# Where the phases of a decoder layer meet: own buffers for one pair of weight blocks, the low parts of A on one engine, four stage buffers, waits by bank, another order of first loads

## The reference

```
z = rmsnorm(h) @ w_in                      # q | k | v | u, 1280 columns
a = windowed attention (8 heads, 2 kv heads, window 128, sinks, T5 bias)
m = pooling means of u over 2/4/8/16 positions, minus u, times w_pool, scaled
h = h + concat(a, m) @ w_out
h = h + (silu(rmsnorm(h) @ w_gate) * (rmsnorm(h) @ w_up)) @ w_down     # d_ff 2816
h = h + sigmoid(rmsnorm(h) @ w_ple_gate) * (p @ w_ple_proj)
```

## Time and profile before

| | |
|---|---|
| runs | 2328.25 us (2327.69 to 2329.66) |
| profiled execution | 2327.3 us, its span 2325.5 us, mean granted clock 0.977 |
| PE busy | 2180.4 us (94%) |
| DVE, ACT, POOL busy | 1369.0, 894.7, 395.6 us |
| edge row phase to FFN half 0 | about 703 to 775 us of the span |
| edge late phase of tile 1 to FFN half 1 | about 1518 to 1577 us |

### The profile page before, as it was taken

One profiled execution on the slowest core, in us unless ns is written; L12 is line 12 of the kernel. 1 busy time (PEld: TensorE's weight loads), 2 busy tenths in 40 slices (PEclk: granted clock), 3 DMA queues, 4 the chain that ended last, 5 costly groups with the idle time before them and its releaser, 6 DMA issues.

```text
span 2325.5 us, 27421 instructions
## 1 busy us (share of the span) xinstructions
PE 2180.4 (94%) x10272; PEld 1812.4 (78%) x10272; DVE 1369.0 (59%) x1909; ACT 894.7 (38%) x1522; POOL 395.6 (17%) x454
## 2 busy tenths in 40 slices
PE   7988989888797899999999999969999999999998
PEld 5777877777685788888888788758888888888887
DVE  4586886886866665555634522666565656354234
ACT  3354554554453333333424421533333334252132
POOL 1434244263424100000000100120000000000000
PEclk9999989999998999999999999989999999999999
DMA  6322425324164323232557453542323235554543
GB/s 172 109 64 55 119 59 151 109 75 116 55 210 132 116 64 100 64 100 64 167 156 189 104 159 100 164 142 76 100 64 100 65 103 169 155 162 127 138 98 91
DMA packets 204447, 265.01 MB, mean 114 GB/s; under 512 B 14859, under 2 KB 128188, under 8 KB 203036
## 3 DMA queue, kind: packets, MB, share of 16 engines
q1 hardware_dynamic: 189456, 219.26, 34.2%
q0 software_dynamic: 12880, 42.51, 5.3%
q10 hardware_dynamic: 1980, 1.50, 0.3%
HBM read 213.41 MB, written 49.80 MB: 113 GB/s over the span
## 4 chain that ended last, share of the span: by engine, by line
PE 77%; DVE 12%; issue 5%; ACT 2%; DMA 2%; POOL 1%; SPq 0%; ACTq 0%; DVEq 0%; POOLq 0%
PE bank L1789 12%; PE bank L1791 12%; PE bank L1790 12%; PE bank L2082 12%; PE bank L2084 12%; PE bank L2086 12%; DVE row_max L1305 1%; DVE scores L1300 1%; PE bank L1815 1%; DVE probsT_lo L1289 1%; DVE w_lo L1185 1%; ACT w_hi L778 1%; PE bank L1806 1%; PE bank L1808 1%; PE bank L1807 1%
## 5 line engine op out<-in xcount | busy, mean ns | idle before, releaser
L1185 DVE TENSOR_TENSOR w_lo<-raw,w_hi 128x1024 fp32r<-128x1024 f32 x200 | 251.9, 1259 | 452.9 <-ACT w_hi L778 451.8
L2082 PE MATMUL bank<-a_hi,ring_hi 128*128 128x512 f32 x1232 | 483.9, 393 | 32.2 <-DVE ring_lo L1498 17.5
L2084 PE MATMUL bank<-a_lo,ring_hi 128*128 128x512 f32 x1232 | 482.5, 392 | 0.0
L2086 PE MATMUL bank<-a_hi,ring_lo 128*128 128x512 f32 x1232 | 482.1, 391 | 0.0
L778 ACT ACTIVATE w_hi<-raw 128x1024 fp32r<-128x1024 f32 x200 | 211.2, 1056 | 450.1 <-PE bank L1791 448.6
L2082 PEld LDWEIGHTS bank<-a_hi,ring_hi 128*128 128x128 f32 x1232 | 233.4, 189 | 81.3 <-DVE ring_lo L1498 17.9
L1789 PE MATMUL bank<-w_hi,hid_hi 128*128 128x512 f32 x704 | 274.8, 390 | 1.2 <-issue 1.2
L1791 PE MATMUL bank<-w_hi,hid_lo 128*128 128x512 f32 x704 | 274.0, 389 | 0.0
L1790 PE MATMUL bank<-w_lo,hid_hi 128*128 128x512 f32 x704 | 273.9, 389 | 0.0
L2086 PEld LDWEIGHTS bank<-a_hi,ring_lo 128*128 128x128 f32 x1232 | 233.3, 189 | 49.0
L2084 PEld LDWEIGHTS bank<-a_lo,ring_hi 128*128 128x128 f32 x1232 | 233.4, 189 | 48.4
(11 more groups left out here) (200 smaller groups left out, 3858.2 us busy)
## 6 DMA issues: line engine op xcount, KB each, us to landing
raw<-in_w_down SPq DMA_DIRECT2D x176, 256.0 KB, 4.0
raws<-in_w_gate SPq DMA_DIRECT2D x88, 256.0 KB, 4.7
raws<-in_w_up SPq DMA_DIRECT2D x88, 256.0 KB, 5.3
hidden_T<-hid POOLq DMA_DIRECT2D x88, 256.0 KB, 2.5
hid_raw<-hidden_T SPq DMA_DIRECT2D x44, 512.0 KB, 5.0
raw<-in_w_in SPq DMA_DIRECT2D x80, 256.0 KB, 4.0
raw<-in_w_out SPq DMA_DIRECT2D x64, 256.0 KB, 4.1
raw<-in_w_ple_gate SPq DMA_DIRECT2D x64, 256.0 KB, 4.1
```

Of the source, the lines that this page charges most:

```text
L1185: nc.vector.tensor_tensor(panel_lo(i), panel_raw(i), panel_hi(i).bitcast(F32), ALU.subtract).then_inc(lo_done, 1)
L2082: mm(dst[:, :], wh[:, g, cols], a_hi[o][:, k, :], start=fresh and k == 0, stop=False, skip_group_check=True)
L2084: mm(dst[:, :], wh[:, g, cols], a_lo[o][:, k, :], start=False, stop=False, skip_group_check=True)
L2086: ins = mm(dst[:, :], wl[:, g, cols], a_hi[o][:, k, :], start=False, stop=k == 3, skip_group_check=True)
```

## The change

1. **First loads.** SP issues panel 0 of w_in after row block 1 instead of after block 3. ScalarE splits it at block 1, ahead of the issues of the constants; copies and low parts of transposed blocks move one block later.
2. **Low parts of A** are all on VectorE, in the order `LO_ORDER = (0, 3, 2, 1, 4, 5, 6)`; `a_rest_pool` goes. A4 and A5 stand in the first pair, at beats 2 and 3.
3. **Four late stage buffers**: tile 3's blocks 2 and 3 get `stage_late`, so all four blocks are normalised in beat 0; ScalarE's four sums of squares stand ahead of beat 0.
4. **Bank-wise waits** on the first products.
5. **Half 1's first pair** has its own buffers; its load is issued after panel `ple_at(1) + 7`, and its first ring entry is made in the last gate panel.

```diff
-N2_IN_FFN = {..., 5: ((3, 0), (3, 1))}
+N2_IN_FFN = {..., 4: ((3, 0), (3, 1))}
+LO_ORDER = (0, 3, 2, 1, 4, 5, 6)
+        raws_first = sb("raws_first", [P, 4, 2, T], WIDE + 16)
+        t1_first = sb("t1_first", [P, 2, T], WIDE)
+        t2_first = sb("t2_first", [P, 2, T], WIDE + 4)
+        p1_first = sb("p1_first", [P, 2, T], ROWS)
+        u2_first = sb("u2_first", [P, 2, T], ROWS + 4)
+        ring_first_hi = sb("ring_first_hi", [P, 2, T], ROWS2, F32R)
+        ring_first_lo = sb("ring_first_lo", [P, 2, T], ROWS2 + 4, F32R)
+        stage_late = sb("stage_late", [P, 2, D], WIDE)
...
 load_pair (SP):
                 elif c == 0:
-                    sp.wait_ge(out_stored, 256)
+                    sp.wait_ge(nT, 48)
+                    sp.wait_ge(panel_used, ple_at(1) + 2)
...
                 else:
                     sp.wait_ge(panel_used, ple_at(1) + PLE_P)
+                    sp.wait_ge(product, 2 * OPS * FPAIRS + 2)
+                if half and c == 2:
+                    sp.wait_ge(out_stored, 256)
+                    sp.wait_ge(hid_done, 4 * FPAIRS + 4)
 late_tile (SP):
+                    if t == 1 and j == 29:
+                        load_pair(1, 0)
 start (SP):
+                if b == 1:
+                    load(Z_AT[0], z_panel(0))
 ring_part_hi (ACT):
                 if m == 0 and half:
-                    act.wait_ge(panel_used, ple_at(1) + PLE_P)
+                    act.wait_ge(lo_done, ple_at(1) + PLE_P)
 ffn_beat (ACT):
+                    if second_start(half, c):
+                        keep = p1_first
+                        act.wait_ge(out_stored, 256)
 start (ACT):
                 if b == 1:
+                    split(0)
                     load_constants()
-                if b == 2:
-                    split(0)
-                if b:
+                if b >= 2:
                     for e in range(2):
-                        i = 2 * b - 2 + e
-                        norm_hi(i, bank[4 + i % 4], wide_hi, e, b - 1)
+                        i = 2 * b - 4 + e
+                        norm_hi(i, bank[4 + i % 4], wide_hi, e, b - 2)
 ffn_beat (DVE):
                 if c == 0 and o == 0:
                     t_sum(half, 0, 0)
                     t_sum(half, 0, 1)
+                    if half == 0:
+                        normalise2_last(0)
+                        normalise2_last(1)
 ffn_section (DVE):
-                            normalise2(3, {1: 0, 3: 2}[o])
-                            normalise2(3, {1: 1, 3: 3}[o])
                         ffn_beat(half, c, o)
+                        if c == 0 and half == 0 and o == 0:
+                            normalise2_last(2)
+                            normalise2_last(3)
+                        if c == 0 and o in (2, 3):
+                            a_rest(half, o + 2)
 late_section (DVE), tile 1, e == 1:
-                        if t == 1 and e == 1 and r in (1, 2, 3):
-                            a_rest(1, (0, 2, 1)[r - 1])
+                        if t == 1 and e == 1 and r in (1, 2):
+                            a_rest(1, (0, 2)[r - 1])
+                            a_rest(1, (3, 1)[r - 1])
+                        if t == 1 and e == 1 and r == 3:
+                            ring_part_lo(1, 0)
 out_section (DVE), tile 3: half 11 gets a_rest(0, 3); ring_part_lo(0, 0) and
 (0, 1) move from ahead of half 15's two add_out to behind them
 product_half (PE):
-                if o == 0 and c == 0 and g == 0:
-                    pe.wait_ge(out_added, 32)
-                    if half:
-                        pe.wait_ge(sig, 16)
+                if o == 0 and c == 0 and half == 0:
+                    pe.wait_ge(out_added, 28 + 1 + 3 * g)
+                if o == 0 and second_start(half, c):
+                    pe.wait_ge(sig, 13 + g)
+                if o == 3 and second_start(half, c):
+                    pe.wait_ge(sig, 16)
```

More of the change, by code:

```diff
@@ L308, in raw_count, with second_start, raws_of, t1_of @@
             return 32 * ((6 if c % 2 == 0 else 5) * half + c // 2 + 1)
+        def second_start(half, c):
+            return half == 1 and c == 0
+        def raws_of(half, c):
+            return raws_first if second_start(half, c) else raws[c % 2]
+        def t1_of(half, c):
+            return t1_first if second_start(half, c) else t1
+        def t2_of(half, c):
+            return t2_first if second_start(half, c) else t2
+        def ring_of(half, m):
+            if half == 1 and m == 0:
+                return ring_first_hi, ring_first_lo
+            return ring_hi[m % 3], ring_lo[m % 3]
+        def ring_source(half, m):
+            c = m // OPS
+            blk, ta, tb = raws_of(half, c), t1_of(half, c), t2_of(half, c)
+            return (blk[:, 0], blk[:, 2], tb[:, :, :], ta[:, :, :], blk[:, 1], tb[:, :, :],
+                    blk[:, 3])[m % OPS]
+        def normed_last(b):
+            return stage[:, b, :] if b < 2 else stage_late[:, b - 2, :]
         def panel_raw(i):
@@ L544, in _ @@
             for half in range(2):
-                load_pair(half, 0)
                 if half == 0:
+                    load_pair(half, 0)
                     store_h1(3)
@@ L719, in ffn_section @@
                         store_hid(half, c, j)
+                        if half == 0 and c == 0 and j == 0:
+                            for b in (2, 3):
+                                store_n2(3, b, 0)
+                                store_n2(3, b, 1)
                 store_hid(half, FPAIRS - 1, 3)
@@ L986, in ring_part_hi @@
                     act.wait_ge(lo_done, ROW_PANELS)
+                    if half:
+                        act.wait_ge(panel_used, ple_at(1) + PLE_P)
                 elif m == 2:
@@ L1055, in ffn_section @@
                     for o in range(OPS):
-                        if c == 0 and half == 0 and o < 2:
-                            for b in (2 * o, 2 * o + 1):
+                        if c == 0 and half == 0 and o == 0:
+                            for b in range(NB):
                                 act.wait_ge(out_added, 24 + 4 + b + 1)
@@ L1211, in normalise2, with normalise2_last @@
                 scale_rows(NORM2[t], b, stage[:, b % 2, :], h_of(t)[:, b, :], g2)
+            def normalise2_last(b):
+                if b < 2:
+                    dve.wait_ge(n2T, 24)
+                else:
+                    dve.wait_ge(panel_used, ROW_PANELS)
+                scale_rows(NORM2[3], b, normed_last(b), h_last[:, b, :], g2)
             def copy_kv(s, b):
@@ L1470, in t_sum @@
                 q = FPAIRS * half + c
-                blk = raws[c % 2]
+                blk, ta, tb = raws_of(half, c), t1_of(half, c), t2_of(half, c)
                 if i == 0:
@@ L1505, in sum_with @@
                 keep = {0: p1, 1: u3, 3: u2}[part]
+                if q == FPAIRS:
+                    keep = {0: p1_first, 1: u3, 3: u2_first}[part]
                 if q or part:
@@ L1726, in out_section @@
                             add_out(t, e, 3)
+                    if t == 3 and half == 15:
+                        ring_part_lo(0, 0)
+                        ring_part_lo(0, 1)
                     hosted("o", t, half)
@@ L2078, in product_half @@
                 fresh = o in (0, 1, 3)
-                wh, wl = ring_hi[m % 3], ring_lo[m % 3]
+                wh, wl = ring_of(half, m)
                 for k in ks:
```

103 lines of the change are left out of this document (42 added, 61 removed).

## The result

| | before | after |
|---|---|---|
| time | 2327.97 us (2327.64 to 2329.66, 4 runs) | 2290.38 us (2289.61 to 2291.70, 4 runs) |
| ratio | | 0.9838, 95% interval 0.9821 to 0.9855 |
| profiled execution | 2327.3 us | 2289.75 us, span 2287.9 us |

The profiled execution lost 37.55 us. The page's busy line of the changed kernel, to be set beside the earlier trace rows: TensorE's work is the same 10272 matmuls, and GpSimd gave six operations to VectorE.

What follows compares the result with a forecast made beforehand. TensorE, 94% busy, was taken as the bound, losing time at two edges by stalls and half clock. Savings of 24.5 + 17.8 - 1.2 = 41.1 us from 2327.3 gave 2286.2, with 0.95 to the median 2287; range 2280 to 2300.

Steps and rivals of the forecast that it cites:

- Edge 1: Row phase into FFN half 0: TensorE's stalls (22.5 us) and slow restarts (7.3) shrink, saving 24.5 us, bounds 20.1 to 26.2.
- Stall 3.1: TensorE's wait before FFN half 0, with A1's subtraction no longer held by GpSimd: 3.1 us instead of 7.8.
- clock 1.7: Loss to TensorE's lowered clock after the wait before FFN half 0: between 0 and 2.4 us, 1.7 taken.
- beat 5: First pair of each half: TensorE's up product stalls on late A6 and u3's copy, 0.5 us half 0, 1.5 half 1.
- the third stall: FFN half 0: TensorE's 6.9 us wait for block 12's load, issued behind tile 3's last scaling, loses its cause.
- Edge 2: Before FFN half 1: 17.5 us stall and 1.8 us restart loss go, 1.5 returns; 17.8 us saved, bounds 13.4 to 19.3.
- Start: First loads: TensorE's first product moves from 18.21 to about 19.6 us, a loss of 1.2 us, between nothing and 6.
- (a): Both first pairs: VectorE becomes the bound, TensorE waits at beat 5, 4.4 us more per half, 2296 us; chance 0.14.
- (b): First loads: panel 0 doesn't land earlier, 4.8 us more, 2292 us; chance 0.06.
- (c): Before FFN half 1: stall stays, early load starves last two gate panels or comes late, 17.8 us more, 2305; chance 0.06.
- (d): Later pair loads: new buffers' waits pass down the queue, 5 us lost per pair, 45 us, 2332 us; chance 0.02.
- The rule beside the row: SBUF: two-input VectorE operations and GpSimd reads take turns; VectorE's longer list delays GpSimd's powers, first rstd up to 2.2 us.

## Why the prediction was right

2287 was forecast (2280 to 2300), 2290.4 measured. The mechanisms of both edges held; the 3.4 us between the two times are nearly all the start. Step by step:

- **Edge 1, 24.5 us forecast, 24.1 measured.** Stall 3.1, measured 2.9; clock 1.7, measured 1.7; beat 5 0.5, measured 0.2. Block 12 was to land at 729; it landed at 734.0, which is 729.5 when the start's 4.5 us are taken off, and VectorE carried A4 and A5 with no wait on it. Two of these are in part luck. The 1.7 was picked between 0 and 2.4; it is 1.7 in all eight profiles in which this wait was 2.85 to 3.99 us, but rows of before could have told both ways (its wait of 2.88 us at 205.10 is followed by a granted clock of 0.67, its wait of 3.00 us at 533.72 by 1.00). And the scalings were to end at 715.6 by seven operations and 1 us of waiting: there are eight, since the second ring part was left out, and no waiting, and they ended at 720.45, which is 716.0 with the same 4.5 us taken off. That the four stage buffers are what removes the third stall is shown (11.0 us back without them), and so is that GpSimd's subtractions cost (6.7 us back with them). No run takes back the order of the last additions and ring parts, or the waits by bank, by itself. A3's low part in half 11 was to end panel 71's split 1 us before TensorE takes it; it ended at 701.4 and there is no wait for it, but no spare time either (TensorE's last wait there ended at 695.96, and a panel takes 5.4 us).
- **Edge 2, 17.8 forecast, 17.8 measured**; beat 5's stall 1.5, measured 1.2. The chain to it held as well: VectorE's sum with block 12 at 1541.7, A6's high part at 1547.3 and the end of u3's copy at 1549.8 were forecast, and came at 1521.90, 1527.56 and 1529.96, or with 19.6 us added at 1541.5, 1547.2 and 1549.6. The sum was right and its reading incomplete. I named GpSimd's subtractions as in the way but gave them no share. Without them, and with the load as late as before, the edge gains 17.8 - 12.4 = 5.4 us; with them, and the load early, 17.8 - 10.7 = 7.1. The two add up to 12.5 of 17.8: 5.3 us came only of both, since each cause stood ready behind the other. At edge 1 the same reckoning gives 13.1 and 17.4, together 6.4 more than the 24.1 that both gave: there part of the gain came with either (the two runs keep the new order of additions and ring parts, so this is no full account of edge 1).
- **Start, 1.2 forecast, 4.5 measured in this profile: the mis-sized term.** The panel was to land at 10.7, by two places at 2.6 us each; it landed at 12.5, and the first product came at 21.1 instead of 19.6. I also let a later wait take some of it back. None did: at 31.97 TensorE waited again for VectorE, 2.5 us where before it waited 1.9. The first product is 2.9 us late, and so is panel 1's split. Of the other 1.6 us, 1.5 stand between panels 1 and 3, where the clock fell in this profile and not in that of before (12.6 us against 11.1). Both lengths were met with either start, so these 1.5 us aren't a fixed price of the change. By medians the new start costs from nothing to 3.7 us in the new kernel and 4.0 in the old one.
- **Rivals.** (a) is refuted for this kernel: beat 5 waits 0.2 and 1.2 us. (b) the panel did land earlier, by 3.3 us. (c) TensorE waited 0.34 us for the split of one of the last gate panels (at 1482.21), exactly as before (at 1501.84), so the early load takes nothing from them. (d) Behind edge 2 the difference stays at 37.5 us, so no later load is held up.
- **The rule beside the row.** That GpSimd and a two-input VectorE operation take turns was borne out in both directions. With GpSimd's subtractions back, VectorE's 1.2 us sums take 5.6 and 5.4 us. VectorE holds up GpSimd in turn, here its powers of tile 3's blocks, three of four at 1.41 to 1.60 us where a free one takes 0.56 (two of four before), at no cost. The prediction put that down to VectorE's longer list, and this isn't borne out: with A4 and A5 back on GpSimd the three take 1.41, 1.60 and 1.47 us all the same. By their times, what they meet are the ring part, the sums and the scalings of beat 0:

```profile
713.34 1.60 POOL L614 TENSOR_TENSOR rstd<-ms,minus_half 128x1 f32<-128x1 f32 x1
```

What stays open: how much of the 4 us by which the row phase differs between executions of one order is chance of DMA landing and how much the clock itself. At the first such place the clock fell where the wait before it was a little longer, but no run here holds the one still while the other moves.

## What to carry to other kernels

A stall names only what came last: at edge 2 either fix alone gives 5 to 7 of 17.8 us, so cost every cause that stands behind a stall, and take them away together. An early load is worth only what the consumer's other operands allow: first put each engine's list in the order in which the first product needs its parts, and count DMA issues on a computing engine as work in the way (the seven here run from 12.54 to 16.25 us, and ScalarE's next operation starts at 16.35). And compare two profiles by the starts of an operation that occurs equally often in both: one table set the start's loss apart from the two gains.

## What the runs showed of the hardware

- At edge 1 a TensorE wait of 2.85 us, and one of 2.4, were followed by 1.2 GHz and a loss of 1.7 us each; waits of 1.2 and 0.9 us there were not. Closing such a wait thus gave more than its length. But the length alone doesn't tell: a wait of 2.44 us at 756.05 with GpSimd's low parts back, and one of 3.00 us at 533.72 in the kernel before, were followed by a granted clock of 1.00.
- The same instructions ran through 30 to 35 us at a granted clock of 1.00 in one execution and 0.66 in another, behind waits of 1.94 and 2.25 us. A difference of under 4 us between two profiles of this kernel's row phase says nothing by itself.
- Two places forward in a queue moved a load's landing by 3.3 us, not by the 5.2 that the spacing of the others gave. Row blocks now landed 5.4 to 12.2 us after issue, where the earlier trace rows had 5.2 to 11.0. The last block, issued at 4.3 us, landed at 16.5, behind half of panel 1 that was issued after it, at 4.8, and landed at 15.4.
